# Sample states' outer products in pairs of heads on three PSUM banks, and one write of each expert's outputs

## What is computed

```
S = jnp.exp(b_last)[..., None] * S + jnp.einsum('bshk,bshv->bhkv', ki * jnp.exp(b_last[:, None] - b), vi)
```

```
for e in range(N_EXPERTS):
    y = y + gates[..., e:e + 1] * swiglu(h, w_gate_up[e], w_down[e])
x = x + g2[:, None, :] * f
```

## Time and profile before

| | us |
|---|---|
| median of three runs | 1584.63 (1581.18 to 1584.77) |
| the profiled execution | 1586.65 |
| its span, first to last instruction | 1584.8 |
| mean granted clock of PE | 0.971 |
| PE busy in the span | 1511.8 (95%) |
| DVE, ACT, POOL busy | 453.1, 326.2, 91.2 |
| read from HBM, written | 521.38 MB, 14.59 MB |

### The profile page before, as it was taken

How to read it: one execution, slowest core, us unless ns; L and a number is a source line. 1 busy time by engine, 2 the same in 40 slices (tenths; PEclk the granted TensorE clock), 3 DMA queues, 4 the chain that set the end, 5 groups by cost and what they waited for, 6 DMA issues and landing times.

```text
span 1584.8 us, 35752 instructions
## 1 busy us (share of the span) xinstructions
PE 1511.8 (95%) x16405; PEld 897.9 (57%) x16405; DVE 453.1 (29%) x703; ACT 326.2 (21%) x505; POOL 91.2 (6%) x133
## 2 busy tenths in 40 slices
PE   6999799999999898799999999999999999999996
PEld 3994588899979657434534435335345344354353
DVE  4653564444577724402010010010020100100212
ACT  3653254343454443300000000000000000000001
POOL 2001010000004300000000000000000000001000
PEclk9999799999999899899999999999999999999996
DMA  9668767994568796999999999999999999999980
GB/s 346 220 213 297 247 214 267 317 315 165 184 214 293 279 405 246 368 361 391 407 417 420 407 413 421 411 414 420 409 418 406 419 417 406 416 419 406 410 361 29
DMA packets 119302, 538.29 MB, mean 340 GB/s; under 512 B 6571, under 2 KB 29225, under 8 KB 89458
## 3 DMA queue, kind: packets, MB, share of 16 engines
q1 hardware_dynamic: 109842, 504.42, 81.1%
q0 software_dynamic: 8368, 28.32, 4.9%
q10 hardware_dynamic: 944, 3.26, 0.6%
HBM read 521.38 MB, written 14.59 MB: 338 GB/s over the span
## 4 chain that ended last, share of the span: by engine, by line
PE 70%; issue 17%; DMA 6%; DVE 4%; ACT 2%; POOL 0%; SPq 0%; ACTq 0%; POOLq 0%; DVEq 0%
PE psum L1256 35%; PE psum L1268 18%; PE psum L852 3%; PE psum L853 3%; PE psum L854 3%; PE psum L770 2%; DMA e_ring<-in_moe_w_gate_up 2%; DMA ring<-in_ada_w 2%; DVE w_lo L1862 1%; PE psum L961 1%; DVE ring L2214 1%; PE psum L817 1%; DMA xe_rows<-h_rows,row_from 1%; PE psum L1269 1%; DMA h<-q_scratch 0%
## 5 line engine op out<-in xcount | busy, mean ns | idle before, releaser
L1256 PE MATMUL psum<-e_ring,xe 128*32 128x512 f32 (+1 forms) x3456 | 337.2, 548 | 2.9 <-DMA e_ring<-in_moe_w_gate_up 2.0
L852 PE MATMUL psum<-hh,w_hi 128*128 128x264 f32 x864 | 253.8, 294 | 17.1 <-DVE w_lo L1862 9.2
L1256 PE MATMUL psum<-ring,xe 128*32 128x384 f32 (+1 forms) x2688 | 251.8, 531 | 0.0
L853 PE MATMUL psum<-hl,w_hi 128*128 128x264 f32 x864 | 248.4, 287 | 0.0
L854 PE MATMUL psum<-hh,w_lo 128*128 128x264 f32 x864 | 248.0, 287 | 0.0
L1256 PEld LDWEIGHTS psum<-e_ring,xe 128*32 128x32 f32 x3456 | 113.0, 111 | 221.2 <-issue 216.1
L1862 DVE TENSOR_TENSOR w_lo<-ring,w_hi 128x1024 fp32r<-128x1024 f32 (+1 forms) x132 | 161.6, 1235 | 145.1 <-ACT w_hi L1463 145.0
L852 PEld LDWEIGHTS psum<-hh,w_hi 128*128 128x128 f32 x864 | 166.3, 192 | 31.2 <-issue 15.8
L1268 PE MATMUL psum<-ring,at 128*32 128x256 f32 x2448 | 180.4, 379 | 0.0
L1269 PE MATMUL psum<-ring,at 128*32 128x256 f32 x816 | 180.0, 379 | 0.0
L1256 PEld LDWEIGHTS psum<-ring,xe 128*32 128x32 f32 x2688 | 87.6, 110 | 159.8 <-issue 159.8
(11 more groups left out here) (402 smaller groups left out, 1214.1 us busy)
## 6 DMA issues: line engine op xcount, KB each, us to landing
e_ring<-in_moe_w_gate_up SPq DMA_DIRECT2D x40, 2048.0 KB, 15.9
ring<-in_moe_w_gate_up SPq DMA_DIRECT2D x24, 2048.0 KB, 19.4
e_ring<-in_moe_w_gate_up SPq DMA_DIRECT2D x32, 1536.0 KB, 14.8
ring<-in_moe_w_gate_up SPq DMA_DIRECT2D x32, 1536.0 KB, 14.7
ring<-in_ada_w SPq DMA_DIRECT2D x20, 2048.0 KB, 11.0
ring<-in_moe_w_down SPq DMA_DIRECT2D x24, 1536.0 KB, 14.7
ring<-in_moe_w_down SPq DMA_DIRECT2D x16, 2048.0 KB, 13.2
e_ring<-in_moe_w_down SPq DMA_DIRECT2D x16, 2048.0 KB
```

What stands on the lines that cost most here:

```text
L852: eng.matmul(to, wh, ah, start=start, stop=False)
L853: eng.matmul(to, wh, al, start=False, stop=False)
L1256: last = eng.matmul(outs[r][s * STRIP:(s + 1) * STRIP, :].rearrange("p (c i) -> p c i", c=4), tokens[:, r * STRIP:(r + 1) * STRIP], pieces ...
```

## The change

It merges two changes and moves one split.

- The outer products go round three banks, 0, 1 and 5, in pairs of heads: pair 2b holds heads 0 and 2 of sample b, pair 2b+1 heads 1 and 3. A pair waits for the update of the pair three places before it, which has the same bank; `s_updated` now counts pairs. DVE's update of a sample is done in two halves, each as soon as its pair is there. Bank 5 held a result of the prompt until `o_scaled` is 1, so pair 2 waits for that.
- The first split of `gla_out` is done earlier on ACT and DVE, before the samples' outputs are finished.
- `expert_gated` and the writes to it are gone, with DVE's `gate_rows` in experts 0 to 6. All gathers read `expert_out`, and the prompt's fetched rows are weighted, added, multiplied by the row of `g2` and added to the stream in four DVE instructions for a tile of 128 tokens, where two stood.

```diff
+OUTER_BANKS = (0, 1, 5)
...
-        expert_gated = nc.dram_tensor("expert_gated", [(NE - 1) * CAP, D], F32)[:]
...
+        def outer_bank(pair):
+            return pb[OUTER_BANKS[pair % len(OUTER_BANKS)]]
...
             for b in range(NB):
-                eng.wait_ge(S["s_updated"], b + 1)
+                eng.wait_ge(S["s_updated"], 2 * b + 2)
                 eng.dma_start(dst[b], s0[b]).then_inc(S[f"s0_moved{b}"], 16)
...
                     send_outputs(expert_out[e * CAP:(e + 1) * CAP, :], y_e)
-                    eng.wait_ge(S["y_g_kept"], 2 * e + 2)
-                    send_outputs(expert_gated[e * CAP:(e + 1) * CAP, :], y_g)
-                    eng.wait_ge(S["y_e_sent"], 64 * (e + 1))
+                    eng.wait_ge(S["y_e_sent"], 32 * (e + 1))
...
-                        eng.indirect_dma_start(back[t][0:TOK[t], c, :], None, expert_gated if t < 2 else expert_out,
+                        eng.indirect_dma_start(back[t][0:TOK[t], c, :], None, expert_out,
...
             def outer(b):
-                if b == 0:
-                    eng.wait_ge(S["kept_act"], 24)
-                    eng.wait_ge(S["k_rows_ready"], 1)
-                else:
-                    eng.wait_ge(S["s_updated"], b)
                 for g in range(GH):
                     rows_g = slice(g * STRIP, (g + 1) * STRIP)
+                    pair = 2 * b + g % 2
+                    if b == 0 and g == 0:
+                        eng.wait_ge(S["kept_act"], 24)
+                        eng.wait_ge(S["k_rows_ready"], 1)
+                    if g < 2 and pair == 2:
+                        eng.wait_ge(S["o_scaled"], 1)
+                    if g < 2 and pair >= len(OUTER_BANKS):
+                        eng.wait_ge(S["s_updated"], pair - len(OUTER_BANKS) + 1)
                     if g >= 2:
                         eng.wait_ge(S["outer_done"], STRIPS * b + g - 1)
-                    last = eng.matmul(pb[g % 2][:, g // 2 * DV:(g // 2 + 1) * DV], k_rows[rows_g, b, :],
+                    last = eng.matmul(outer_bank(pair)[:, g // 2 * DV:(g // 2 + 1) * DV], k_rows[rows_g, b, :],
...
             def outputs_s(b):
-                eng.wait_ge(S["s_updated"], b + 1)
+                eng.wait_ge(S["s_updated"], 2 * b + 2)
...
-                    eng.wait_ge(S["y_g_kept"], 2 * NE - 1)
+                    eng.wait_ge(S["y_g_kept"], 1)
...
-            def first_splits(kind):
-                for m in range(AHEAD):
+            def first_splits(kind, first=0):
+                for m in range(first, AHEAD):
...
             ada_copy(9)
+            split(UNIT_AT["gla_out", 0], late=True)
             eng.wait_ge(S["os_done"], STRIPS * NB)
...
-            first_splits("gla_out")
+            first_splits("gla_out", 1)
...
             def update_s(b):
                 eng.wait_ge(S[f"s0_moved{b}"], 16)
-                eng.wait_ge(S["outer_done"], STRIPS * (b + 1))
                 s = s0[b]
-                for g in range(GH):
-                    last = eng.scalar_tensor_tensor(s[:, g, :], s[:, g, :], ea[:, g, b:b + 1], pb[g % 2][:, g // 2 * DV:(g // 2 + 1) * DV],
-                                                    ALU.mult, ALU.add)
-                last.then_inc(S["s_updated"], 1)
+                for a in range(2):
+                    eng.wait_ge(S["outer_done"], STRIPS * b + 3 + a)
+                    for g in (a, a + 2):
+                        last = eng.scalar_tensor_tensor(s[:, g, :], s[:, g, :], ea[:, g, b:b + 1],
+                                                        outer_bank(2 * b + a)[:, g // 2 * DV:(g // 2 + 1) * DV], ALU.mult, ALU.add)
+                    last.then_inc(S["s_updated"], 1)
...
             roots(2, 2 * GH, 2 * GH + 1)
+            split(UNIT_AT["gla_out", 0], late=True)
             eng.wait_ge(S["os_turned"], 1)
...
                 def early(t):
-                    to = x_tok[:, t, :] if t < 2 else back[2][0:n, 1, :]
...
-                        link(eng.scalar_tensor_tensor(to, back[t][:, 1, :], w_early[:, 1, t:t + 1], to, ALU.mult, ALU.add))
-                    eng.scalar_tensor_tensor(to, back[t][0:n, 0, :], w_early[0:n, 0, t:t + 1], to, ALU.mult, ALU.add).then_inc(S["x_final"], 1)
...
+                    first, second = back[t][:, 0, :], back[t][:, 1, :]
+                    link(eng.tensor_scalar(second, second, w_early[:, 1, t:t + 1], None, ALU.mult))
+                    link(eng.scalar_tensor_tensor(first, first, w_early[:, 0, t:t + 1], second, ALU.mult, ALU.add))
+                    link(eng.tensor_tensor(first, first, row_bc[:, 0, :], ALU.mult))
+                    eng.tensor_tensor(x_tok[:, t, :], x_tok[:, t, :], first, ALU.add).then_inc(S["x_final"], 1)
...
                     one_expert(it)
                     keep_rows(it * 2 + 4)
-                    eng.wait_ge(S["y_e_kept"], it + 1)
-                    gate_rows().then_inc(S["y_g_kept"], 1)
```

More of the change, by code:

```diff
@@ L2393, in early @@
                     n = TOK[t]
[L2394 removed]
                     eng.wait_ge(S[f"y_back{t}"], 32)
                     if t == 2:
+                        to = back[2][0:n, 1, :]
                         link(eng.tensor_scalar(to, to, w_early[0:n, 1, t:t + 1], None, ALU.mult))
[L2398 to L2400 removed]
+                        eng.scalar_tensor_tensor(to, back[2][0:n, 0, :], w_early[0:n, 0, t:t + 1], to,
+                                                 ALU.mult, ALU.add).then_inc(S["x_final"], 1)
+                        return
+                    first, second = back[t][:, 0, :], back[t][:, 1, :]
[3 more added lines that the diff above has]
+                    eng.tensor_tensor(x_tok[:, t, :], x_tok[:, t, :], first, ALU.add).then_inc(S["x_final"], 1)
                 def one_expert(it, between=((), ())):
```

3 lines of the change are left out of this document (1 added, 2 removed).

## The result

| | before | after |
|---|---|---|
| median, us | 1584.63 (1580.77 to 1587.54, 5 runs) | 1570.60 (1568.55 to 1575.85, 5 runs) |
| ratio, 95% interval | | 0.9929 (0.9906 to 0.9952) |
| the profiled execution, its span | 1586.65, 1584.8 | 1569.80, 1567.6 |
| mean granted clock | 0.971 | 0.980 |
| PE, DVE, POOL busy | 1511.8, 453.1, 91.2 | 1504.5, 443.7, 83.2 |

The change is faster by 11.2 us (7.6 to 14.9). As a difference, 9.2 us were forecast, and the interval of the 11.2 measured holds them.

A forecast was written before the change was run, and what follows sets the result against it. PE was taken to set the pace in the experts, with DMA just keeping up, and PE and DVE to alternate in the sample states; 5.6 + 1.3 + 2.3 = 9.2 us gave 1575.4, range 1570.4 to 1580.6.

The forecast's parts named there:

- Change 1: Stage of the sample states: outer products on three banks shorten PE's waits and may keep its clock; 5.6 us forecast.
- I take one stretch as left: 5.6 us: Stage of the sample states: one of two stretches at 1.2 GHz stays; 5.6 us gained, ends 2.8 and 8.5.
- the two cases: Stage of the sample states: one slow stretch left gives 5.6 us; PE keeping 2.4 GHz gives 8.5.
- The argument for a stretch: Stage of the sample states: outer products stay narrow, 32 rows of the array at a time, so one slow stretch remains.
- The third pause "with no fall in it": Stage of the sample states: a pause of PE at 172 us without a clock fall, used for leaving one slow stretch.
- That PE keeps 2.4 GHz: Rival, stage of the sample states: no slow stretch, 8.5 us there, 12.1 in all, 1572.5; chance 0.29.
- That both stretches return: Rival, stage of the sample states: both 1.2 GHz stretches come back, 2.8 us there, 6.4 in all, 1578.3; chance 0.23.
- PE staying slow into gla_out: Rival: PE stays at 1.2 GHz from 148 us into gla_out; slower, 16 us more giving 1591.1; chance 0.03.
- Change 2: Start of gla_out: its first split done earlier lets PE start sooner; 1.3 us, range 0.9 to 1.6.
- Change 3: Experts: one write each removes DMA bytes, so expert 7's waits for weight tiles go; 2.3 us, ends 0 and 2.3.
- the waits did not stay: Rival: expert 7's waits stay because the earlier gather meets the same tiles; 6.9 us in all, 1577.7; chance 0.08.
- loads do not bound them: Rival: loads bound the experts, so the writes' whole 6.7 us come off; 13.6 in all, 1571.0; chance 0.03.

The follow-up runs named there:

- filled pauses: The kernel before, waits untouched, with three extra unread matmuls of 128 rows in each of the three 1.25 us pauses of PE: 1579.21 us, ratio 0.9978.
- narrow filling: The kernel before with three extra unread matmuls in each of the three pauses of PE, of 32 rows instead of 128: 1579.47 us, ratio 0.9977.
- two banks in pairs: The changed kernel with its outer products in pairs on banks 0 and 1 instead of three banks: 1575.61 us, ratio 0.9943.
- single write alone: The kernel before with only the single write of each expert's outputs: 1578.18 us, ratio 0.9970.
- split alone: The kernel before with only the first split of gla_out moved ahead: 1581.78 us, ratio 0.9989.
- banks alone: The kernel before with only the three banks and the halved updates: 1576.24 us, ratio 0.9958.
- both fillings: The kernel before with extra unread matmuls in PE's three pauses, once of 128 rows (1579.21 us) and once of 32 (1579.47 us).
- warm: The changed kernel with extra unread transposes of a constant in six idle times of PE: 1568.13 us, ratio 0.9903.
- best: The changed kernel with unread transposes in nine idle times of PE and the writes of the experts' outputs issued by SP: 1564.75 us, ratio 0.9880.

## Why the prediction came out as it did

**Change 1: right in kind, too small.** At full clock the last update was to end 19.1 us behind outer product 2 (168.0 less 148.88); it ended 18.51 behind it, 9.06 less than before where 8.5 was forecast. The mechanism holds: the waits became 0.45 us, as forecast (0.4). By the filled pauses the 9.06 divide into 5.4 of clock and 3.6 of waits (27.57, 22.14 and 18.51 us), where the prediction had 5.7 and 2.8. The step that failed is "I take one stretch as left: 5.6 us". In five of eight profiles none was left; alone the part gave 6.9 us (4.3 to 9.0), between the two cases. The argument for a stretch, that the products stay narrow work, found no support in the narrow filling, under which the clock stayed up to 172.5, or in the five profiles; that three of eight fell inside such a product leaves it a part. The third pause "with no fall in it" was weak evidence against the pauses: two of three pauses had a fall, so that one makes a fall likely and not certain.

**The rivals on the clock.** That PE keeps 2.4 GHz (1572.5) had 0.29 and is what the profile shows; it should have had the largest share. That both stretches return is what two banks in pairs did, not three. PE staying slow into gla_out did not come. The Trainium skill, page "TensorE: Matmul & The Clock Gate", section "A second HAM failure mode: psum-queue depth-cycling", tells of a PE that goes round PSUM banks and idles briefly between its groups of matmuls, often enough for its clock to fall and rise. The two-bank profiles with their pauses agree (10.24 to 13.65 us at 0.50); the same two banks with their pauses filled show 0 and 1.66, and three banks ran a whole stage at 1.00 five times of eight, so a round of banks by itself did not bring it.

**Change 2: right.** 1.3 forecast, 1.58 in the profile (1.57 alone: 8.81 to 7.24); gla_out waited for no tile or store, but for the samples' low part (L2156 in the timeline). Its time alone (1.4, -0.6 to 4.0) shows nothing by itself.

**Change 3: the waits right, an item missing.** Expert 7 gave 2.46 us, forecast 2.3, by the mechanism named: bytes, back with the bytes and not with the writes. Its longest landing is 21.2 us, forecast about 20. The rows were read rightly as a queue that grows: the medians now stay at 13.2 and 13.6 from expert 1 to 6. The gather starts 11.0 us into expert 7 (1438.85 less 1427.84), before 13.6 (1453.74 less 1440.16): 2.6 earlier, forecast 3 to 4. The two passes more cost 1.9 us a tile, and were hidden. The step that failed is the sum: it counted the removed DMAs by their bytes alone, and with 14 fewer on POOL its drain is also 1.14 us shorter, on the path to the end in every profile. 2.46 and 1.14 make 3.6 of the 5.0 us measured alone (2.1 to 7.6). The remaining 1.4 is within that interval, and the profile of the single write alone has 1.27 us of it as the later fall of the clock in the tail. Rivals: the waits did not stay, and experts 1 to 6 are still 109.37 us each, so loads do not bound them. By the figure in the section "Specifications" of the Trainium skill's page "DMA: Bandwidth & Descriptors" (about 358 GB/s) they would; expert 6 moves 411 GB/s after the change too, and the measurement decides.

**What no step of the prediction gives.** In the two profiles 1.86 and 0.98 us lie around the start of the experts, where before has 17.07 us at 0.50 between 635 and 680 us and the changed kernel 10.24, which it has in its second run too. But split alone and the kernel that writes twice have 17.07, banks alone, the single write alone and both fillings 10.24: the parts do not order them, and I count this as chance. The later fall of the clock in the tail, worth 1.28 us, may be the change's own. In the six profiles of kernels that write every row twice the clock falls 1.2 to 2.1 us behind the start of the placement five times and 4.4 once (the narrow filling); in the other eight it falls 2.7 to 3.4 us behind it seven times and 1.5 once (warm). No run tried it by itself. Both pieces help to make the difference of the two profiles (16.9 us) larger than that of the medians (14.0 in the first set, 11.0 in the second).

**The sum by what was measured**: 6.9 and 1.4 and 5.0 make 13.3 us, against 9.2 forecast; the whole together gave 11.2 (7.6 to 14.9). The times cannot place a difference of this size. By the profiles the terms that were too small are the clock (a stretch too many) and change 3 (the drain, and what the tail's clock adds).

## What to carry to other kernels

Where PE waits a microsecond here and there, read the granted clock of that stretch before pricing the wait: here the waits were worth 3.6 us and the clock they cost 5.4, and unread work in the same pauses brought the clock back without moving a wait in the code. A queue whose landings grow from loop to loop is near its limit; here some 1% of the bytes taken off it (0.39 of about 45 MB an expert) removed waits that showed only in the last loop. Cut both profiles at the same instructions before naming a cause, and run each part alone: a piece that differs between two profiles and that no part moves is no gain of the change.

## What was not expected of the hardware

- PE's extra work in its idle times held the granted clock at 1.00 (with 128 rows) or 0.96 (with 32) over a stage that otherwise shows 0.75, and best takes 1564.75 us where the changed kernel takes 1570.60 to 1572.19, with more instructions on PE.
- The clock also fell where no idle time of PE stands in the trace: 3 of 8 profiles of the stage on three banks have 3.41 to 6.83 us at 0.50, and each us of it makes the stage 0.46 to 0.49 us longer.
- POOL's drain at the end takes 5.302 us in kernels that issue 64 or 78 DMAs on it and 6.445 in those that issue 92, whatever their bytes.
- One core kept 411 to 414 GB/s over whole experts.
